# Log-forget pages of a paged-attention decoder step: 64 row fetches and a turn on TensorE instead of 64 column fetches

## The reference, cut to what matters

```python
def gather(pool):
    g = pool[page_table]                       # (8 sequences, 8 pages, 128 tokens, 8 heads)
    return g.reshape((B, g.shape[1] * g.shape[2]) + pool.shape[2:])

lf_all = jnp.concatenate([gather(cache_lf).astype(jnp.float32), logf], axis=1)
cum = jnp.cumsum(lf_all, axis=1)
s = jnp.einsum('bqhd,bkhd->bhqk', q, k) * ATTN_SCALE
s = s + (cq[..., :, None] - ck[..., None, :])  # differences of cum
```

## Time and profile before

| | |
|---|---|
| runs, us | 2674.87, 2678.24, 2674.41 |
| profiled execution, span | 2673.7 us; of its own time nothing else is recorded, and the three runs lie 0.7 to 4.5 us above the span |
| TensorE (PE) busy | 2522.4 us, 94% |
| its weight loads (PEld) | 2321.7 us, 87% |
| VectorE (DVE) busy | 1159.7 us, 43% |
| ScalarE (ACT) busy | 919.7 us, 34% |
| GpSimd (POOL) busy | 44.6 us, 2% |
| mean granted TensorE clock | 0.962 |
| slowest kind of matmul, L503 on adax | 512 of 534 ns |
| DMA, mean over the span | 230 GB/s |

### The profile page before, as it was taken

How to read it: one execution, slowest core, us unless ns; L and a number is a source line. 1 busy time by engine, 2 the same in 40 slices (tenths; PEclk the granted TensorE clock), 3 DMA queues, 4 the chain that set the end, 5 groups by cost and what they waited for, 6 DMA issues and landing times.

```text
span 2673.7 us, 53818 instructions
## 1 busy us (share of the span) xinstructions
PE 2522.4 (94%) x20995; PEld 2321.7 (87%) x20995; DVE 1159.7 (43%) x1767; ACT 919.7 (34%) x1155; POOL 44.6 (2%) x86
## 2 busy tenths in 40 slices
PE   6898999999999999899999777797999999999999
PEld 3597999999999999799997343597999999999999
DVE  0343444444444445666652111255444544454444
ACT  1432323233333334566541112245333333333332
POOL 0130000000000000000000000000000000000000
PEclk7798999999999999999999878898999999999999
DMA  8887777777767764344456999943444444454444
GB/s 355 341 313 230 286 267 286 275 283 267 289 219 281 277 230 162 128 157 150 164 210 256 389 361 408 349 161 125 161 168 165 165 165 165 159 171 165 165 159 159
DMA packets 105867, 614.13 MB, mean 230 GB/s; under 512 B 16192, under 2 KB 16464, under 8 KB 56128
## 3 DMA queue, kind: packets, MB, share of 16 engines
q1 hardware_dynamic: 101728, 603.81, 61.5%
q0 software_dynamic: 4064, 9.26, 1.3%
HBM read 604.36 MB, written 8.66 MB: 229 GB/s over the span
## 4 chain that ended last, share of the span: by engine, by line
PE 87%; DMA 8%; SPq 2%; DVE 1%; ACT 1%; issue 1%; ACTq 0%; DVEq 0%
PE banks L562 26%; PE banks L563 25%; PE banks L564 25%; PE banks L503 4%; DMA adax<-in_w_ada_dram 2%; PE banks L830 1%; PE banks L787 1%; DMA adaw<-in_w_ada_dram 1%; SPq L440 1%; DMA kv_raw<-in_vpool_dram 1%; PE banks L514 1%; DMA raw<-in_w_dram 1%; PE banks L649 1%; PE banks L661 0%; PE banks L773 0%
## 5 line engine op out<-in xcount | busy, mean ns | idle before, releaser
L562 PE MATMUL banks<-h_hi,w_hi 128*128 128x288 f32 x3792 | 1129.1, 298 | 28.6 <-DVE h_lo L1127 23.1
L563 PE MATMUL banks<-h_lo,w_hi 128*128 128x288 f32 x3792 | 1122.6, 296 | 0.0
L564 PE MATMUL banks<-h_hi,w_lo 128*128 128x288 f32 x3792 | 1121.2, 296 | 0.0
L1095 DVE TENSOR_TENSOR w_lo<-raw,w_hi 128x1024 fp32r<-128x1024 f32 (+2 forms) x666 | 763.8, 1188 | 378.7 <-ACT w_hi L867 372.4
L867 ACT ACTIVATE w_hi<-raw 128x1024 fp32r<-128x1024 f32 (+2 forms) x666 | 667.8, 1030 | 554.0 <-PE banks L564 507.3
L562 PEld LDWEIGHTS banks<-h_hi,w_hi 128*128 128x128 f32 x3792 | 717.0, 189 | 50.2 <-issue 43.7
L563 PEld LDWEIGHTS banks<-h_lo,w_hi 128*128 128x128 f32 x3792 | 716.9, 189 | 0.8
L564 PEld LDWEIGHTS banks<-h_hi,w_lo 128*128 128x128 f32 x3792 | 716.3, 189 | 0.0
L562 PE MATMUL banks<-g_hi,w_hi 128*128 128x288 f32 x1376 | 409.2, 297 | 0.0
L563 PE MATMUL banks<-g_lo,w_hi 128*128 128x288 f32 x1376 | 406.8, 296 | 0.0
L564 PE MATMUL banks<-g_hi,w_lo 128*128 128x288 f32 x1376 | 406.6, 296 | 0.0
(11 more groups left out here) (186 smaller groups left out, 1134.7 us busy)
## 6 DMA issues: line engine op xcount, KB each, us to landing
raw<-in_w_dram SPq DMA_DIRECT2D x172, 1024.0 KB, 4.8
adaw<-in_w_ada_dram SPq DMA_DIRECT2D x112, 1024.0 KB, 6.4
raw<-in_w_dram SPq DMA_DIRECT2D x64, 896.0 KB, 4.6
raw<-in_w_in_dram SPq DMA_DIRECT2D x49, 1024.0 KB, 4.8
adax<-in_w_ada_dram SPq DMA_DIRECT2D x32, 1024.0 KB, 8.3
raw<-in_w_dram SPq DMA_DIRECT2D x32, 960.0 KB, 4.7
raw<-in_w_out_dram SPq DMA_DIRECT2D x16, 1024.0 KB, 4.8
kv_raw<-in_kpool_dram SPq DMA_DIRECT2D x24, 512.0 KB, 6.0
```

Source lines behind the costliest of these rows:

```text
L562: pe.matmul(bank[:, 0:T], hi, m_hi[:, k, :], start=k == 0, stop=False)
L563: pe.matmul(bank[:, 0:T], hi, m_lo[:, k, :], start=False, stop=False)
L564: last = pe.matmul(bank[:, 0:T], lo, m_hi[:, k, :], start=False, stop=k == nk - 1)
L1095: dve.tensor_tensor(w_lo[:, r, a:b], raw[:, r, a:b], w_hi[:, r, a:b].bitcast(F32), ALU.subtract).then_inc(S["lo_ready"], 1)
```

## The change

Each page is fetched as one whole row, 4096 bytes, to partition i of a new tile `lfrow` (64 pages x 1024 values), which lies where `v_new` is put later. The loop on POOL is written out, 64 times, with constant positions of the page entry and of the target. Behind the down segment of the first chunk TensorE waits for all 64 loads and turns the rows, one head at a time (64 pages x 128 tokens, taken with a step of 8 values), into bank 5; VectorE then waits for the eight turns and copies the bank (128 x 512) into `lfc`, with heads and pages exchanged. The later reader waits for this copy instead of the loads. The store of `rev` stays behind the 64 loads in POOL's queue.

```diff
--- before.py
+++ after.py
@@ -210,6 +210,7 @@
         rbr = sb("rbr", [P, HEADS])
         v_new = sb("v_new", [TS, 2 * HEADS * HD])
         vn0 = top[0] - 2 * HEADS * HD * 4
+        lfrow = at("lfrow", [NB * PAGES, PAGE * HEADS], F32, vn0)
         ohr = at("ohr", [32, REV], F32, vn0 + 4096)
         adr = at("adr", [HEADS, REV], F32, vn0 + 5632)
 
@@ -275,7 +276,7 @@
         names = """ld_small ld_x w_landed0 w_landed1 hi_ready lo_ready w_used acc_a_read acc_b_read ada_landed0
             ada_landed1 adax_landed0 adax_landed1 adax_landed2 adax_landed3 ada_used ada_sb ada_sel ada_fin
             c_ready sq_ready sq_used y0_ready hf_ready hhi_ready hn_ready gain_ready h_ready g_ready
-            act_chain dve_chain y_stored heads_stored v_stored ss_read ld_att ld_rel ld_selw ld_pages
+            lfc_sum lfc_ready act_chain dve_chain y_stored heads_stored v_stored ss_read ld_att ld_rel ld_selw ld_pages
             lf_landed rev_sum rev_ready rev_stored toe_landed fa_ready fe_ready lf_ready hsq_ready hss_ready
             hy_ready head_ready lft_sum lft_ready ncum_sum ncum_ready p_s p_max p_exp p_scaled p_v p_vcopy
             p_t p_tcopy p_o p_high p_low vn_sum vn_ready kv_landed0 kv_landed1 kv_landed2 kv_first_landed
@@ -463,9 +464,9 @@
             for q in range(NS):
                 pool.dma_start(rbr[32 * q:32 * q + 32, :], relb).then_inc(S["ld_att"], 16)
             pool.wait_ge(S["ld_pages"], 16)
-            with pool.Fori(0, NB * PAGES) as i:
-                pg = pool.value_load(pages[0:1, bass.ds(i, 1)], min_val=0, max_val=POOL - 1)
-                pool.dma_start(lfc[:, bass.ds(i, 1), :], lfpool[bass.ds(pg, 1), :, :].rearrange("a p h -> p a h"))\
+            for i in range(NB * PAGES):
+                pg = pool.value_load(pages[0:1, i:i + 1], min_val=0, max_val=POOL - 1)
+                pool.dma_start(lfrow[i:i + 1, :], lfpool[bass.ds(pg, 1), :, :].rearrange("a p h -> a (p h)"))\
                     .then_inc(S["lf_landed"], 16)
             pool.wait_ge(S["rev_ready"], 1)
             pool.dma_start(rev_dram, rev[:, :].unsqueeze(1).to_broadcast([HEADS, P, REV])).then_inc(S["rev_stored"], 16)
@@ -637,6 +638,17 @@
                         run(seg, pe, lambda i, seg=seg: pair(seg, i), 1)
                     if seg.squares:
                         sum_squares(seg)
+                    if seg is ffn1[1]:
+                        turn_log_forget()
+
+            def turn_log_forget():
+
+                pe.wait_ge(S["lf_landed"], 16 * NB * PAGES)
+                rows = lfrow[:, :].rearrange("a (p h) -> a p h", h=HEADS)
+                for h in range(HEADS):
+                    last = pe.transpose(bank[5][:, h * NB * PAGES:(h + 1) * NB * PAGES], rows[:, :, h],
+                                        ident[0:NB * PAGES, 0:NB * PAGES])
+                last.then_inc(S["lfc_sum"], 1)
 
             segments(ffn1)
 
@@ -1255,6 +1267,10 @@
                     else:
                         run(seg, dve, lambda i, seg=seg: body(seg, i, (seg, i - 1)), 1, ch, LINKS[seg.kind])
                     late = seg, seg.bodies - 1
+                    if seg is ffn1[1]:
+                        dve.wait_ge(S["lfc_sum"], 1)
+                        dve.tensor_copy(lfc[:, :, :].rearrange("p a h -> p h a"),
+                                        bank[5].rearrange("p (h a) -> p h a", h=HEADS)).then_inc(S["lfc_ready"], 1)
                 r = 1 if seg in ffn1 else 2
                 if seg.squares:
                     splits(split_low, r, -2)
@@ -1357,7 +1373,7 @@
                 p_low(t)
 
 
-            dve.wait_ge(S["lf_landed"], 16 * NB * PAGES)
+            dve.wait_ge(S["lfc_ready"], 1)
             dve.wait_ge(S["lft_ready"], 1)
             dve.tensor_copy(lfn_w[:, :].rearrange("p (j h q) -> p j h q", j=GB, q=NS),
                             lft[0:TS, 2, :].unsqueeze(1).unsqueeze(3).to_broadcast([TS, GB, HEADS, NS]))
```

## The result

The changed kernel takes 2683.6 us (median of 20 runs, 2672.99 to 2688.23), the kernel before 2677.64 us (median of 20, 2669.24 to 2684.49). The medians lie 6.0 us apart; the ratio over all runs, on which the text goes, is 1.0019, 95% interval 1.001 to 1.0027: 5.1 us slower, between 2.7 and 7.2. The forecast was 2676.2 (2671.5 to 2680.2) with 0.83 on "no difference". The time lies above the range, and the change made the kernel slower.

The account below looks back on a forecast made before the run. TensorE, busy 94% of the span, was taken as the bound, with one 13.9 us stall behind the rev store. Terms 1.1 + 0.2 + 0 + 0 + 0 = +1.3 us gave 2676.2 us, range 2671.5 to 2680.2.

Parts of the forecast that it names:

- Item 5: Rev store issued earlier, at about 191: ada loads behind it still 10 to 14 late; no difference, bounds -3 and +3.
- table of landings: SP loads behind the rev store land 15.2, 27.1, 34.2 and 38.4 us after its issue, read from the old profile.
- Item 4: POOL's written-out page loop: 0.3 us saved a round, 19 us in all (8 to 61), store out at about 191.
- Item 1: Eight turns on TensorE behind the first chunk's last down body, with no idle time to hide them: +1.1 us.
- Item 2: VectorE's half splits queue behind turns and copy, so TensorE waits at the segment end: +0.2 us, bounds 0 and 0.9.
- Items 3 and 6: SP's reloads delayed behind VectorE's splits, covered by three microseconds: 0; fewer small DMA pieces in page loads: 0.
- Faster: Rival: with row loads the rev store streams in 6.2 us and the stall goes; 2662.3 us, chance 0.08.
- Slower: Rival: weight stream breaks at the new wait, second chunk's up segment, ada load 4.4 late; 2682.6 us, chance 0.09.
- Loop no shorter: Rival: writing out POOL's loop saves nothing, store stays near 210 with the same stall; 2676.2 us, chance 0.15.

Follow-up runs that it names:

- e12: Kernel before, POOL made to wait until body 6 is done, so the rev store goes out at the start of body 7; 2680.07 us.
- e1: Changed kernel, POOL made to wait so that the rev store goes out about 5 us into its body; 2679.88 us, ratio 1.0011.
- e3: Changed kernel with the rev store cut into sixteen pieces, one a body; 2666.1 us, ratio 0.9954.
- e8: Changed kernel, unchanged, run again for a second profile; 2680.24 us.
- e4: Kernel before with the rev store cut into sixteen pieces, one a body; 2666.17 us, ratio 0.996.
- e5: Kernel before with POOL's 64 column loads written out, no rows or turns; 2679.66 us, ratio 1.0006.
- e9: Kernel before, unchanged, run again for a second profile; 2671.05 us.
- e10: Kernel before with POOL's 64 column loads written out, run again for a second profile; 2683.55 us.

## Why the prediction was wrong

**Item 5 failed: "10 to 14 of lateness wherever it falls".** The mechanism was right (same store, same stall, an ada pair late). The table of landings held for three loads: read off at 188.5 it puts the pair at 215.6 and 222.7 and the next raw tile at 226.9; they came at 215.2, 222.8 and 227.0. But it was worked out only at 191.2, at 192 and from 197 to 200, and not from 186 to 190, where it gives 222.7 - 207.4 = 15.3. What a few points gave was taken for all places, when POOL's saving was known no better than 8 to 61 us, a spread of three bodies and more. Lateness measured 15.4, slow clock 3.0 for the 2.0 taken. The table is wrong, too, for a load right behind the store: the raw tile issued with it should have come at 203.7 and came at 193.9, which hurt nothing here. It does count at 191.2, where the ada pair itself is next behind the store and item 5 has it 11 to 12 late. Its place there is 1.2 us into the body, and the nearest run, e12 at 0.8, has that pair in time and the next one 8.8 late, a loss of 10.9 where item 5 works out 13 to 16. So "10 to 14" broke at both ends, at 8.8 and at 15.4; by e12, a store at the 191 foretold would have lost some 3 us less than before (an estimate from one profile). With two profiles each, the place costs +3.0 where 0 stood, on the very edge of the -3 to +3. Among the ten places the loss is 16.8 on average from 11.6 to 13.2 us and 14.7 from 4.95 to 6.05, +2.1. The signs show the same: the long pair took 48.8 where 42 to 47 stood, and TensorE was idle for 14.3 where 8 to 14 stood.

**Item 4 mis-sized** the round: 0.37 saved for the 0.3 taken. Over 63 rounds that is 4.4 us more; the loop also starts 1.8 later, so the store went out 2.5 earlier than the 191 foretold. Harmless by itself, it moved the store into the part of the body that item 5 had left out.

**Item 1 right**: 1.04 for 1.1. **Item 2** right in kind: the copy is 1.10, not the 0.68 of L1391, which does not exchange two dimensions in its output (no run tells that from the other differences between the two); TensorE waits 0.5 (0.48 in the row), not 0.2, inside the bound of 0.9. Together 1.53 for 1.3. The same 15.50 and 15.7 stand in the profiles of e1, e3 and e8, and the old 14.48 and 15.20 in those of e4 and e5, which turn nothing. **Items 3 and 6 right**: the ada loads behind the new wait land within 10.1 with no wait on them, though with 1.6 us of cover instead of 3, and the smaller pieces were covered (15.21 before and after).

The terms as measured, 3.0 + 1.53 = 4.5, lie inside the 2.7 to 7.2 that the times show. The experiments show each in the profile; in the times they show the stall's size (-11 us without it) and nothing finer, so how the measured 5.1 splits between place and turns rests on the profiles. A further 2.8 of the miss in microseconds is the base: the three runs shown first had a median of 2674.87, twenty have 2677.64.

**The rivals.** "Faster" failed as its row said: the store lands in 37.2, rows or columns. "Slower" was right in sign and wrong in place: nothing broke at 489; the slowdown came from the stall already known. "Loop no shorter" is out by 21.7 us.

The two profiled spans differ by 12.8 us. The place and the turns explain about 6; most of the rest lies in the attention part, whose code the change leaves alone. TensorE's first loads of `lfr` and last of `pst` (count, shortest, median and longest in ns, first and last start), in the changed kernel and then in the unchanged kernel run again (e9):

```profile
L785 PEld LDWEIGHTS banks<-big,lfr x32: 186/190/333, 1443.0 to 1541.6; 128*128 128x128 f32 x32
...
L842 PEld LDWEIGHTS banks<-kv_z,pst x48: 106/110/177, 1669.2 to 1733.7; 128*32 128x32 f32 x48
```

```profile
L773 PEld LDWEIGHTS banks<-big,lfr x32: 186/190/192, 1436.8 to 1529.3; 128*128 128x128 f32 x32
...
L830 PEld LDWEIGHTS banks<-kv_z,pst x48: 106/110/178, 1653.5 to 1718.1; 128*32 128x32 f32 x48
```

That is 290.7 and 281.3 us. The kernel before had 284.7 in its first profile, and its version with the loop written out, which has no turns, 290.2 (e10). So the same code scatters over 9 us here; what sets it stayed open. The change is not what sets it: over all fourteen profiles, first and repeated, this stretch takes 287.1 us on average in the six of the changed kernel and its variants and 286.8 in the eight of the kernel before and its variants.

## What to carry to other kernels

When an edit moves a transfer that collides with a periodic stream, work out the loss over the whole period, not at the one or two places where the move is expected to end: here it ran from 10.9 to some 17 us with the place, and the place was uncertain by several periods. A stall that is carried along is also the thing to remove: cutting one long store into sixteen, a piece a body, was worth 11 us, twice what the change cost. And look for such a cause in the queue behind the lines being edited, since the loads that were changed cost nothing before or after.

## What the runs showed of the hardware

A store of 1.5 MB from 8 partitions took 37.2 us and from 16 partitions 18.7, with like pieces, and loads of 1 MB on another queue landed up to 29.4 us after their issue beside the first in the changed kernel, where their median is 4.8 to 6.4. A load issued 0.17 us behind that store (changed kernel) or 0.5 us behind it (e12) landed in 5.2 and 5.1, one issued 1.0 us behind it in 14.2 (kernel before) and 16.9 (e8); no run shows why. After 16.6 us of which TensorE was idle for 14.3, the next 17.35 us ran at a mean granted clock of 0.82 and not at 1.00, which cost 3.0. Writing out POOL's loop took 0.36 to 0.37 us off a round of 1.51, more than the 0.13 of the three instructions that the sequencer's rows showed for the loop.
